# Delta-rule heads: decay and column scalings on ScalarE, level 0 of the inverse per head between the projection units

## What is computed

```python
g = jnp.cumsum(g.reshape(Bn, N, C, H).transpose(0, 3, 1, 2), axis=-1)
decay = jnp.exp(jnp.where(lower_incl, g[..., :, None] - g[..., None, :], -jnp.inf))
k_beta = k * beta[..., None]
v_beta = v * beta[..., None]
m = jnp.where(strict, jnp.einsum('bhncd,bhnsd->bhncs', k_beta, k) * decay, 0.0)
rhs = jnp.concatenate([v_beta, k_beta * jnp.exp(g)[..., None]], axis=-1)
sol = lax.linalg.triangular_solve(m + jnp.eye(C, dtype=jnp.float32), rhs, left_side=True, lower=True,
                                  unit_diagonal=True)
intra = jnp.where(lower_incl, jnp.einsum('bhncd,bhnsd->bhncs', q, k) * decay, 0.0)
```

## Time and profile before

| | us |
|---|---|
| median of 3 runs | 2711.45 |
| lowest and highest of them | 2707.46, 2714.69 |
| the profiled execution, whole time | 2714.07 |
| its span in the trace | 2712.3 |
| busy: TensorE, VectorE, ScalarE, GpSimd | 2604.7, 1582.2, 1088.5, 111.4 |

### The profile page before, as it was taken

One profiled execution on the slowest core, in us unless ns is written; L12 is line 12 of the kernel. 1 busy time (PEld: TensorE's weight loads), 2 busy tenths in 40 slices (PEclk: granted clock), 3 DMA queues, 4 the chain that ended last, 5 costly groups with the idle time before them and its releaser, 6 DMA issues.

```text
span 2712.3 us, 34398 instructions
## 1 busy us (share of the span) xinstructions
PE 2604.7 (96%) x11814; PEld 2069.0 (76%) x11814; DVE 1582.2 (58%) x2021; ACT 1088.5 (40%) x1474; POOL 111.4 (4%) x101
## 2 busy tenths in 40 slices
PE   7899999999899999999999989999899989899998
PEld 5657888887668888886678868888676878688886
DVE  5545755756456746656887554344559885543444
ACT  5554433435454424432444442223424534422323
POOL 1000000000000000000110010000101100100000
PEclk9999999999999999999999999999999989999998
DMA  4202332333103333342220123333222201233332
...
DMA packets 394583, 208.01 MB, mean 77 GB/s; under 512 B 9738, under 2 KB 392660, under 8 KB 394484
## 3 DMA queue, kind: packets, MB, share of 16 engines
...
## 4 chain that ended last, share of the span: by engine, by line
PE 89%; DVE 7%; ACT 2%; issue 1%; DMA 0%; POOL 0%; DVEq 0%; SPq 0%; ACTq 0%; POOLq 0%
PE ps L604 64%; PE ps L623 6%; PE ps L1164 2%; PE ps L880 1%; PE ps L1174 1%; DVE ps L2638 1%; DVE x_sb L2641 1%; PE ps L1034 1%; PE ps L1049 1%; PE ps L1184 1%; DVE yc L2379 1%; ACT lnt L1385 1%; ACT whi L1381 1%; PE ps L855 1%; PE ps L890 1%
## 5 line engine op out<-in xcount | busy, mean ns | idle before, releaser
L1381 ACT ACTIVATE whi<-raw 128x1024 fp32r<-128x1024 f32 (+1 forms) x354 | 395.7, 1118 | 1086.6 <-PE ps L604 969.6
L604 PE MATMUL ps<-h_hi,whi 128*128 128x512 f32 x1984 | 788.4, 397 | 4.7 <-ACT whi L1381 4.1
L604 PE MATMUL ps<-h_lo,whi 128*128 128x512 f32 x1984 | 773.2, 390 | 0.0
L604 PE MATMUL ps<-h_hi,wlo 128*128 128x512 f32 x1984 | 530.3, 389 | 0.0
L1982 DVE TENSOR_TENSOR wlo<-raw,whi 128x1024 fp32r<-128x1024 f32 (+1 forms) x354 | 460.4, 1301 | 49.0 <-ACT whi L1381 48.0
L604 PEld LDWEIGHTS ps<-h_hi,whi 128*128 128x128 f32 x1984 | 373.2, 188 | 89.3 <-ACT whi L1381 7.7
L604 PEld LDWEIGHTS ps<-h_lo,whi 128*128 128x128 f32 x1984 | 373.0, 188 | 82.1 <-issue 5.7
L604 PEld LDWEIGHTS ps<-h_hi,wlo 128*128 128x128 f32 x1984 | 372.4, 188 | 77.3
L604 PE MATMUL ps<-a_hi,whi 128*128 128x512 f32 x592 | 230.3, 389 | 0.0
L604 PE MATMUL ps<-a_lo,whi 128*128 128x512 f32 x592 | 230.3, 389 | 0.0
L2673 DVE TENSOR_TENSOR cv<-ps,rstd 128x512 f32<-128x512 f32 x88 | 60.9, 692 | 249.0 <-PE ps L604 241.0
...
## 6 DMA issues: line engine op xcount, KB each, us to landing
...
```

The costliest lines, as they stand in the source:

```text
L604: return pe.matmul(ps[:, ACC[s], :], w[s][:, k, :], r[:, k, :], start=start, stop=stop)
L1381: act.activation(whi[s][:, 0:kt, :], raw[s][:, 0:kt, :], ACT.Copy).then_inc(w_hi_ready.sem, 1)
```

## The change

For each head, ScalarE's new `head_scaled` replaces VectorE's two operations on the gap, its three column scalings and the four-column copy, 16 ScalarE instructions of 128x128 with a per-partition pointer operand (four `Relu`, twelve scalings) and a small copy; the two exponentials stay where they are. Level 0 of a head's inverse leaves the loop: VectorE masks directly into `xT` at the end of `head_ended`, TensorE transposes that in `head_turned` into bank STAT[1], the bank in which `qk` is also formed, and VectorE's `head_turned` makes both differences. For heads 0 and 1 this stands after units 24 and 25, for head 2 after the last unit, for head 3 behind the first two level-1 products. The product `qk` of head h now waits for `x0_new` of head h-1. The loop is shorter by 4 (24 in place of 28), and `lt` takes the buffer `kb`. Ten late taps stand behind the preparation of heads 0 (two), 1 (four) and 2 (four), the other six in the loop; each now waits for the operation before it.

The diff, cut to its core (what is left out: declarations, the renumbered waits of ScalarE's part of the loop and of the layer norm, and the buffer `lnr`):

```diff
                     pe.wait_ge(kb_ready.sem, kb_ready.at(L, h))
                     if h >= 1:
-                        pe.wait_ge(head_ready.sem, head_ready.at(L, h - 1))
+                        pe.wait_ge(intra_made.sem, intra_made.at(L, h - 1))
                     for tb in range(TB):
                         mm = pe.matmul(ps[:, STAT[0], tb * P:(tb + 1) * P], gk[:, h, tb * P:(tb + 1) * P],
                                        kb[:, h % 2, tb * P:(tb + 1) * P], start=True, stop=True)
                     mm.then_inc(kk_ready.sem, 1)
+                    if h >= 1:
+                        pe.wait_ge(x0_new.sem, x0_new.at(L, h - 1))
                     for tb in range(TB):
                         mm = pe.matmul(ps[:, STAT[1], tb * P:(tb + 1) * P], gk[:, h, tb * P:(tb + 1) * P],
                                        gq[:, h, tb * P:(tb + 1) * P], start=True, stop=True)
                     mm.then_inc(qk_ready.sem, 1)
+
+                def head_turned(h):
+
+                    pe.wait_ge(lt0_ready.sem, lt0_ready.at(L, h))
+                    for tb in range(TB):
+                        c = slice(tb * P, (tb + 1) * P)
+                        mm = pe.transpose(ps[:, STAT[1], c], xT[:, h, c], ident[:])
+                    mm.then_inc(p0_ready.sem, 1)
...
                     if i >= N_IN2 - GH:
                         h = i - (N_IN2 - GH)
+                        if h >= 2:
+                            head_turned(h - 2)
                         if h >= 1:
                             head_products(h - 1)
                         head_in(h)
+                head_turned(GH - 2)
                 head_products(GH - 1)
...
+                    if n == 0:
+                        pe.wait_ge(eg_ready.sem, eg_ready.at(L, GH - 1))
+                    elif n == 1:
+                        pe.wait_ge(kb_ready.sem, kb_ready.at(L, GH - 1))
+                    else:
+                        pe.wait_ge(p1_kept.sem, p1_kept.at(L, n - 2))
+                    if n >= GH:
+                        pe.wait_ge(xt_kept.sem, xt_kept.at(L, n - GH))
...
-                pe.wait_ge(head_ready.sem, head_ready.at(L, GH - 1))
-                for n in range(GH * LEVELS + 1):
-                    if n < GH * LEVELS:
+                for n in range(STEPS + 1):
+                    if n < STEPS:
                         level_first(n)
-                    if n == 19:
+                    if n == 1:
+                        head_turned(GH - 1)
...
-                    if n >= GH + 1:
+                    if n >= 1:
                         level_second(n - 1)
...
+
+                def head_scaled(h):
+
+                    e = h % 2
+                    act.wait_ge(grow_ready.sem, grow_ready.at(L, h))
+                    if h >= 2:
+                        act.wait_ge(intra_made.sem, intra_made.at(L, h - 2))
+                        act.wait_ge(gq_scaled.sem, gq_scaled.at(L, h - 2))
+                    for tb in range(TB):
+                        c = slice(tb * P, (tb + 1) * P)
+                        order.step(act.activation(dm[:, e, c], ps[:, ROT[0], c], ACT.Relu, scale=-1.0, bias=cols["gc"][:, tb, h:h + 1]))
+                    order.told(act.activation(eg[:, e, :], ps[:, ROT[0], :], ACT.Exp), eg_ready, L, h)
+                    order.settle()
+                    order.told(act.activation(dm[:, e, :], dm[:, e, :], ACT.Exp, scale=-1.0), decay_ready, L, h)
+                    if h == 0:
+                        act.wait_ge(beg_ready.sem, beg_ready.at(L, 0))
+                    act.wait_ge(kT_ready.sem, kT_ready.at(L, h))
+                    for dst, by in ((kbeg, "beg"), (kout, "egl")):
+                        for tb in range(TB):
+                            order.step(act.activation(dst[:, h, tb, :], ps[:, TRN[0], tb * P:(tb + 1) * P], ACT.Identity,
+                                                      scale=cols[by][:, tb, h:h + 1]))
+                    act.wait_ge(gvT_ready.sem, gvT_ready.at(L, h))
+                    for tb in range(TB):
+                        ins = act.activation(vb[:, h, tb, :], ps[:, TRN[1], tb * P:(tb + 1) * P], ACT.Identity, scale=cols["beta"][:, tb, h:h + 1])
+                        if tb < TB - 1:
+                            order.step(ins)
+                        else:
+                            order.told(ins, turned_used, L, h)
+                    order.step(act.activation(eg_last[:, h, :], eg[:, e, CH - 1::CH], ACT.Copy))
...
                     if i >= N_IN2 - GH:
                         h = i - (N_IN2 - GH)
-                        act.wait_ge(gap_ready.sem, gap_ready.at(L, h))
-                        if h >= 2:
-                            act.wait_ge(head_ready.sem, head_ready.at(L, h - 2))
-                            act.wait_ge(gq_scaled.sem, gq_scaled.at(L, h - 2))
-                        order.told(act.activation(eg[:, h % 2, :], ps[:, ROT[0], :], ACT.Exp), eg_ready, L, h)
-                        order.told(act.activation(dm[:, h % 2, :], dm[:, h % 2, :], ACT.Exp), decay_ready, L, h)
+                        head_scaled(h)
...
                 def head_begun(h):
 
-                    s = h % 2
-                    dve.wait_ge(grow_ready.sem, grow_ready.at(L, h))
-                    order.settle()
-                    order.step(dve.tensor_tensor(by_token(dm[:, s, :]), by_token(ps[:, ROT[0], :]), column("gc", h), ALU.subtract))
-                    order.settle()
-                    order.told(dve.tensor_scalar(dm[:, s, :], dm[:, s, :], 0.0, None, ALU.min), gap_ready, L, h)
                     dve.wait_ge(brow_ready.sem, brow_ready.at(L, h))
-                    order.told(dve.tensor_tensor(kb[:, s, :], ps[:, ROT[1], :], gk[:, h, :], ALU.mult), kb_ready, L, h)
-                    dve.wait_ge(kT_ready.sem, kT_ready.at(L, h))
-                    order.step(dve.tensor_tensor(kbeg[:, h, :, :], by_token(ps[:, TRN[0], :]), column("beg", h), ALU.mult))
-                    order.step(dve.tensor_tensor(kout[:, h, :, :], by_token(ps[:, TRN[0], :]), column("egl", h), ALU.mult))
-                    dve.wait_ge(gvT_ready.sem, gvT_ready.at(L, h))
-                    order.told(dve.tensor_tensor(vb[:, h, :, :], by_token(ps[:, TRN[1], :]), column("beta", h), ALU.mult), turned_used, L, h)
+                    order.settle()
+                    order.told(dve.tensor_tensor(kb[:, h % 2, :], ps[:, ROT[1], :], gk[:, h, :], ALU.mult), kb_ready, L, h)
 
                 def head_ended(h):
 
                     s = h % 2
                     dve.wait_ge(decay_ready.sem, decay_ready.at(L, h))
                     dve.wait_ge(kk_ready.sem, kk_ready.at(L, h))
-                    order.settle()
                     order.step(dve.tensor_tensor(gv[:, h, :], ps[:, STAT[0], :], dm[:, s, :], ALU.mult))
                     dve.wait_ge(qk_ready.sem, qk_ready.at(L, h))
+                    dve.wait_ge(turned_used.sem, turned_used.at(L, h))
                     order.told(dve.tensor_tensor(intraT[:, h, :], ps[:, STAT[1], :], dm[:, s, :], ALU.mult), intra_made, L, h)
-                    dve.wait_ge(eg_ready.sem, eg_ready.at(L, h))
-                    order.settle()
-                    order.told(dve.tensor_copy(eg_last[:, h, :], eg[:, s, CH - 1::CH]), head_ready, L, h)
-
+                    order.settle()
+                    order.told(dve.tensor_tensor(by_token(xT[:, h, :]), by_token(gv[:, h, :]),
+                                                 lev[:, 0, :].unsqueeze(1).to_broadcast([P, TB, P]), ALU.mult), lt0_ready, L, h)
+
+                def head_turned(h):
+
+                    dve.wait_ge(p0_ready.sem, p0_ready.at(L, h))
+                    order.settle()
+                    order.step(dve.tensor_tensor(by_token(gk[:, h, :]), unit_blocks, by_token(ps[:, STAT[1], :]), ALU.subtract))
+                    order.told(dve.tensor_tensor(by_token(xT[:, h, :]), unit_blocks, by_token(xT[:, h, :]), ALU.subtract), x0_new, L, h)
+
+                def level_masked(n):
+
+                    if n >= 2:
+                        dve.wait_ge(p1_ready.sem, p1_ready.at(L, n - 2))
+                    order.settle()
+                    order.told(dve.tensor_tensor(by_token(lt[:, n % 2, :]), by_token(gv[:, n % GH, :]),
+                                                 lev[:, 1 + n // GH, :].unsqueeze(1).to_broadcast([P, TB, P]), ALU.mult), lt_ready, L, n)
+
...
+                LATE = ((0, 2), (2, 6), (6, 10), (10, 10))
+
+                def late_tap(n):
+                    k, t = TAPS_IN + n // NC, n % NC
+                    order.settle()
+                    ins = dve.scalar_tensor_tensor(yc[:, t, :], ypad[:, t, k:k + SEQ], param(pd, L, D_DW + k * NC + t), yc[:, t, :],
...
                     if i >= N_IN2 - GH:
                         h = i - (N_IN2 - GH)
+                        if h >= 2:
+                            head_turned(h - 2)
                         if h >= 1:
                             head_ended(h - 1)
                         head_begun(h)
```

(16 more changed lines are left out.)

122 lines of the change are left out of this document (55 added, 67 removed).

## The result

| | before | changed |
|---|---|---|
| median of 8 runs each, us | 2714.56 | 2705.5 |
| lowest and highest | 2707.46, 2715.57 | 2699.28, 2708.5 |
| the profiled execution, its span | 2714.07, 2712.3 | 2704.91, 2703.1 |

The ratio is 0.9971, with an interval of 0.996 to 0.9983. The changed kernel is 0.3% faster: 7.9 us of 2711.45 by the ratio. The forecast was 2705 (2696 to 2716), no difference above 0.3% at 0.60, faster at 0.34. The time came within 0.5 us of it, and the ratio lies at the bound between the two cases, just inside the likelier one. The gain itself was forecast at 6.6 us; it is 7.9 by the ratio and 9.1 by the two medians. The forecast took it from the median of three runs of the kernel before, 2711.45, while that of all eight is 2714.56.

What follows compares the result with a forecast made beforehand. TensorE, with 89% of the chain, was taken as the bound. Per layer, 10.2 us gained in B less 3.4 in A and 3.5 for the clock gave 3.3, two layers 6.6: from 2711.45 to 2705 us, range 2696 to 2716.

Steps and rivals of the forecast that it cites:

- The wait in A: TensorE waits 3.0 us between the units, ahead of `qk` of head 1, for `x0_new` of head 0.
- A: Stretch of the heads between units, once per layer; the last unit was to end 3.4 us later at full clock.
- The small operations: ScalarE's 128x128 operations with pointer operand: 0.26 us each in a row, bounds 0.16 and 0.37.
- B: Stretch from the last unit's end to the third level-1 product, once per layer: 28.6 us, to shrink by 10.2.
- The clock: TensorE's granted clock falls behind the new waits, costing 1.5 us in A and 2.0 in B, 3.5 per layer.
- about 0.5 behind each wait: Sign expected in the new profile: granted clock at about half of full speed somewhere behind each TensorE wait.
- rival 1: The waits do not lower the clock: gain of 6.8 us per layer, time 2698; chance 0.20.
- the count at full clock: Per layer, 10.2 us gained in B less 3.4 lost in A: 6.8 us, before any loss of clock.
- whatever VectorE does: In the steady loop TensorE sets the time per n, so removing ten taps there is worth nothing.
- Rival 2: ScalarE becomes the bound at 0.34 to 0.37 us per small operation; gain vanishes, 2709 to 2712; chance 0.16.
- A half clock that stays: From the wait in A on TensorE stays at half speed: 4.8 us lost per layer, 2721; chance 0.06.
- an order that does not bring the heads forward: `qk` waits for `x0_new` in each head, head 3 ends as late as before: 2709 to 2716; chance 0.06.

Runs made afterwards that it cites:

- fill_waits: Changed kernel with dummy TensorE products filling the waits ahead of `qk` of heads 1 and 2 and the second level-1 product: 2700.57 us, ratio 0.9959.
- taps_in_loop: Changed kernel with eight of the ten taps between the units put back into the loop: 2704.39 us, ratio 0.997.
- pool_later: Changed kernel with level-0 differences first, masks ahead of `intraT`, head 3 transposed in STAT[0], head 3's GpSimd operations after the loop's sixth product: 2693.3 us, ratio 0.9923.
- diff_first: Changed kernel with level-0 differences of heads 0 and 1 ahead of the scaling and weight split behind units 24 and 25: 2694.33 us, ratio 0.9939.
- scale_on_vector: Changed kernel with the three column scalings back on VectorE, decay and copy staying on ScalarE: 2711.24 us, ratio 0.9996.
- masks_only_b: Changed kernel with masks ahead of `intraT`, head 3 transposed in STAT[0], head 2's level-1 mask before head 3's differences: 2702.81 us, ratio 0.9958.

## Why the prediction was right

**The wait in A.** I had 3.0 us ahead of `qk` of head 1, and it was 2.69 and 2.70, released by line 2473 as named. The 0.3 us that I had added for GpSimd were not paid by VectorE: the mask of head 0 began at 2147.63, GpSimd's operation 0.05 later, and that one took 1.80 instead of 1.26. ScalarE reached its delayed weight split 10.67 us after head 0's gate rows (2144.01 less 2133.34); my count gave 10.75. With 0.44 for the transposes and the clock, A grew by 5.0 and 4.8; I had 3.4 and 1.5, which is 4.9. With no half clock (fill_waits) A is 3.5 longer than before, where I had 3.4.

**The small operations.** 0.25 us apart, and the last of four 0.37 to 0.44 long (1.12 to 1.19 less three times 0.25); I had taken 0.26 apart and 0.37 long. The figures of the Trainium skill ("ScalarE: Activation LUTs", What ACT_TABLE_LOAD costs) gave 0.29, an estimate; the measurement decides, and it is below that.

**B.** Counted from the end of the last unit in layer 2 (2166.28), at full clock throughout: low part and differences done at 3.6 (predicted 3.8), ScalarE's `vb` at 11.1 (11.3), the level-1 mask at 14.3 (14.7), the third product at 18.16 (18.4). The terms that I wrote down for ScalarE add up to 11.1, not to the 11.3 that I went on with; without that slip the third product comes at 18.2. `intraT` of head 3 was released by `vb`. The shrinking of 10.2 is 82.3 less 72.1 in the layer that lost no clock; up to the third product alone it is 10.4 (28.6 less 18.2).

**The clock.** I had 1.5 in A and 2.0 in B per layer. By fill_waits it was 1.6 and 2.0 in layer 1, 1.4 and 0 in layer 2. The step was right in size where the clock fell. In the second layer's B it did not fall, although the waits were as long, so that the sign "about 0.5 behind each wait" failed there; rival 1 had allowed for such a case, and why it was this layer no run shows. The net gain is 3.2 and 5.3 us where I had 3.3 twice. This sums to 8.5, and the spans differ by 9.2, against a forecast of 6.6. The remaining 0.7 lies outside these stretches, where single executions differ too: the stretch from 1281.78 that stood at 0.50 before is at 1.00 in the changed kernel's trace.

**What was luck.** That 2705 and 2705.5 lie so close is in part luck. The forecast started from 2711.45, 3.1 us under the median of all eight runs, and gained 2.5 us too little by the medians; the two errors nearly cancel. What the traces bear out is the count at full clock, 6.8 us per layer against 6.7, and the price of the clock where it fell.

**What was wrong, or only half seen.** First, the prediction said that the loop costs TensorE its own time "whatever VectorE does". This holds for taps (taps_in_loop), not for GpSimd's operations: pool_later shows 0.9 us of waits per layer there. It touched no term of the sum. Second, I had read the change's price in A as belonging to it. It came from two differences standing behind 1.9 us of work that could wait (diff_first: 8.7 us less than the changed kernel by the two ratios, 11.2 by the two medians, 10.5 by the four stretches). Third, before its run I took ScalarE's part alone for 2 to 4 us; it brings 5.1 of about 8 to 9.

**The rivals.** A clock that holds gives 2700.6 (fill_waits) and not 2698. By the four stretches rival 1 had the gain right, 13.4 us where it said 13.6; by the ratio of fill_waits it is 11.1. Its time was too low also because it started from 2711.45; how much of the 2.6 us is due to that, the runs do not separate. Rival 2, ScalarE as the bound, needed 0.34 to 0.37 us per small operation, and 0.25 was measured. VectorE does wait for ScalarE's `vb` in head 3 (0.67 us), as my count had it, but giving the scalings back to VectorE costs 5.7 us (scale_on_vector), and taking `vb` out of the masks' way gains 1.3 us of B in layer 2 (masks_only_b). A half clock that stays, and an order that does not bring the heads forward, did not occur in any trace.
